# Five placeholder entries taken out of the order of work of a hybrid decoder step

## The chip, the cores and the metric

The kernel runs on one core of a Trainium2 chip. Its time is the device time of one execution, in microseconds (us). Five engines work side by side, each in the order of its own list of instructions: TensorE (PE, matrix products), VectorE (DVE), ScalarE (ACT), GpSimd (POOL, which here issues the gathers) and SyncE (SP, which issues the loads of weights). They wait for each other by semaphores.

## The reference

One layer is computed for 576 tokens: 512 of a new sequence (the prompt) and 8 tokens each of 8 running sequences (the sample, 64 tokens). All numbers are float32.

- Mixer: z = x·w_in + b_in is cut into u, q, k, v and two gates. u goes through a state-space scan (S5), a GELU and a gated linear unit (GLU). q, k and v go through attention over a window of 128 keys. The two branches, each times the sigmoid of its gate, are added and multiplied with w_out.
- A layer norm of (alpha·x + mixer) gives x1.
- PEER, the channel mixer: each token makes 8 queries (x1·peer_wq), scores each against two sets of 128 keys, takes the best 16 pairs per head, and so has 128 experts of 16384. For each expert e it computes a = gelu(U[e]·x1)·gate and adds a·V[e]. U[e] and V[e] are rows of 1024 numbers, of the token's own choice.
- A second layer norm of (alpha·x1 + PEER) gives the output.

Each of the 576 tokens needs its own 128 rows of U and 128 rows of V.

## The kernel before

The tokens lie in five tiles: tile 0 is the sample (64 tokens), tiles 1 to 4 are the prompt (128 tokens each). They are worked in the order 1, 0, 2, 3, 4. Group 0 is tiles 0 and 1, group 1 is tiles 2, 3 and 4: the mixer runs once for each group.

PEER goes by slots. A slot is one expert of each of the 128 tokens of a tile: a gather of 128 U rows and a gather of 128 V rows (524 KB each). Tile 0 folds its 64 tokens twice into 128 partitions and so has 64 slots; the others have 128, together 576. For slot q:

- POOL issues the gather of U rows and, four slots behind, that of V rows (`u_row`, `v_row`, lines 683 and 696), each into a place of a ring. In slots 72 to 191 of the whole row of slots the ring of U has 6 places and that of V has 6. POOL waits until the place's former row has been used. Its instructions run in order, so a V gather that waits holds up the U gathers behind it.
- DVE forms the dot products with x1 (line 1513). After every fourth slot ACT does the GELU and DVE multiplies with the gate (`gated`, line 1482).
- The V row is weighed and added in one of two ways: ACT builds a diagonal matrix (line 1804) and PE multiplies it with the row (`weigh`, line 1038), or DVE adds it alone (`add_row`, line 1501, the first of a tile line 1497). `rows_on_vector` chooses which.

Two slots are a half-step, an item `("peer", t, c)` of tile t. While the slots of tiles 1 and 0 are worked (192 slots, 96 half-steps), the mixer of group 1 and the choice of experts of later tiles are worked between them. This is the mixed stage. Half-steps are counted through here, 0 to 63 for tile 1 and 64 to 95 for tile 0. After it only PEER of tiles 2 to 4 is left, with little between.

The order of the mixed stage is written in `schedule` as a list `mix` of entries, and spread by a planned cost: `COST` holds for every kind of item a time on DVE and one on PE. All costs of `mix` and `tops` are added and divided by `SPREAD` (184 slots); an entry goes in as soon as the costs placed so far, with half of its own, are within this rate times the number of slots. `("wait",)` is an entry that no engine has a function for: it does nothing, costs 4.0 in the sum, and so leaves about a slot free of mixer work.

From that one list each engine takes its own order. On PE `mixer_first` puts the items that follow a half-step ahead of that half-step's products with V rows. On DVE `half_steps_behind` puts items behind by a number of half-steps (`VECTOR_BEHIND`): `qkv` and `merge` by 2, `drain_wo` and `ln` by 1. On ACT most are one behind.

The items that matter here, in their order:

- `qkv` t: products for q, k, v (line 841 on PE), then bias and rotary embedding on DVE (lines 1219 to 1231). `turn` t: PE turns q and k over (lines 849, 852), and waits for the rotary embedding; ACT copies the results out of the banks (line 1574). `s`, `p`, `pt`, `pv`: attention (lines 900, 910, 920 on PE).
- `gs`, `ga`, `merge` m, for eight m: gates, GLU and the branch of attention (line 933 on PE, lines 1319 to 1330 on DVE).
- `wo` k, for eight k: the product with w_out for tiles 2 and 3 in four banks (line 961). The first waits until DVE has done the last merge. `drain_wo` (line 1358) adds a finished bank to x on DVE. `wo_last` 4: the two halves of tile 4 (line 971); the first goes into the bank of `wo` 2,0 and waits until DVE has drained it.
- `ln` t (lines 1339 to 1352), `xt` t: PE turns x1 over (line 981) and waits for `ln` t. `wq` h, for eight h: the queries (line 990); they need all three `xt`.
- `last` 1: DVE's sum of the rows that it added is folded into the bank by PE (line 1052). `final` 1: the second norm of tile 1 on DVE (lines 1538, 1339 to 1352).

Of the kernel before, what the change touches and what calls it, by code (L numbers as in the profile page):

```python
# [93 lines left out]
def schedule():  # L94

    gates = lambda m: [("gs", 0, m), ("ga", 0, m)]
    s = [("tables",), ("u",), ("ut",), ("uc",), ("qkv", 0), ("ca", 0), ("qkv", 1), ("ca", 1), ("wt",),
         ("turn", 0), ("turn", 1), ("ws",), ("rec",), ("k", 0), ("k", 1),
         ("ss",)] + gates(0) + gates(1) + gates(2) + gates(3)
# [3 lines left out]
    wo = lambda t, hf: [("wo_last", t, hf), ("drain_wo", t, hf)]  # L103
# [4 lines left out]
    first = [[("top", 1, 2)], [("top", 1, 3)], [("choose", 1, 1), ("sc", 1, 2)], [("index", 1, 1)]]  # L108
    first += [[("top", 1, h)] for h in range(4, 8)] + [[("choose", 1, 2)], [("index", 1, 2), ("sc", 0, 0)]]
    parts = [(j, kv) for j in range(1, 4) for kv in range(2)]  # L110
    attention = [[("qkv", 2)], [("qkv", 3)], [("qkv", 4)], [("wait",)], [("turn", 2), ("turn", 3), ("turn", 4)], [("s", *parts[0])], [("p", *parts[0]), ("s", *parts[1])]]
    for n in range(1, len(parts)):
        attention.append([("pt", *parts[n - 1]), ("p", *parts[n])])
        attention.append([("pv", *parts[n - 1])] + ([("s", *parts[n + 1])] if n + 1 < len(parts) else []))
# [1 line left out]
    mix = [first[0], attention[0], first[1], first[2], attention[1], first[3]]  # L116
    first, attention = first[4:], attention[2:]
# [3 lines left out]
            mix.append(first[n])  # L121
    for m in range(8):
        mix += [[("gs", 1, m)], [("ga", 1, m)], [("merge", 1, m)]]
    mix += [[("wait",)]] + [[("wo", k)] for k in range(8)]
    mix += [[("drain_wo", 2, 0), ("drain_wo", 2, 1)], [("wait",)], [("wo_last", 4, 0)], [("ln", 2)], [("wo_last", 4, 1)]]
    mix += [[("drain_wo", 3, 0), ("drain_wo", 3, 1)], [("ln", 3)], [("drain_wo", 4, 0), ("drain_wo", 4, 1), ("xt", 2)], [("ln", 4)], [("xt", 3)]]
    mix += [[("wait",)], [("wait",)], [("wait",)], [("xt", 4)], [("wait",)]] + [[("wq", 1, h)] for h in range(8)]
    mix += [[("sc", 2, 0), ("sc", 2, 1)], [("wait",)]] + [[("top", 2, h)] for h in range(2)] + [[("choose", 2, 0)], [("index", 2, 0)]]
    tops = [[("top", 0, h)] for h in range(4)] + [[("choose", 0, 0), ("sc", 0, 1)], [("index", 0, 0)]]
    tops += [[("top", 0, h)] for h in range(4, 8)] + [[("choose", 0, 1)], [("index", 0, 1), ("fold",)]]  # L130
# [171 lines left out]
class Plan:  # L302
# [3 lines left out]

    def __init__(self):
        self.items = schedule()
        self.on_vector = rows_on_vector(self.items)
        self.filled, self.drained, self.before, self.bank = {}, {}, {}, {}  # L310
# [1632 lines left out]
```

## Time and profile before

| what | value |
|---|---|
| median of 3 runs | 2052.76 us (2048.89 to 2058.01) |
| profiled execution | 2049.74 us, span 2047.9 us |
| PE busy | 1589.3 us, 78% of the span |
| DVE busy | 1246.9 us, 61% |
| POOL busy | 1229.6 us, 60% |
| ACT busy | 439.3 us, 21% |
| read from HBM | 669.71 MB, 329 GB/s over the span |
| mean granted clock of PE | 0.866 of full speed |

"Busy" is the time in which an engine executes an instruction; issuing, waiting for semaphores and branching are not counted. The DMA share is the mean busy share of the core's 16 DMA engines. A matrix product in float32 with 128x128 weights and 512 columns appears as two instructions. One V row (one slot) on PE is two such products, one for each half of the 1024 columns, so four instructions of line 1038.

### The profile page before, as it was taken

To read this page: it belongs to the slowest core of one execution; us is meant where nothing else is said; L and a number is where in the kernel's file an instruction comes from. 1 tells how busy PE (TensorE), PEld (TensorE's weight loads), DVE (VectorE), ACT (ScalarE), POOL (GpSimd) and SP (SyncE) were. 2 spreads that over 40 slices of the span, in tenths; PEclk is the share of its full clock that TensorE was granted. 3 is DMA by queue.
4 is the path that set the end of the run, shared out by engine and by line. 5 is a ranking of instruction groups with operands and counts; after the bars stand their busy time and mean duration, and the time that the engine had idled before them with its cause. 6 is when DMAs were issued, how large, how long until landed. Compare 5 with 4: busy or idle time off the path is not lost.

```text
span 2047.9 us, 17225 instructions
## 1 busy us (share of the span) xinstructions
PE 1589.3 (78%) x4837; PEld 797.7 (39%) x4837; DVE 1246.9 (61%) x3135; ACT 439.3 (21%) x1035; POOL 1229.6 (60%) x1370
## 2 busy tenths in 40 slices
PE   7988887889989797973757767848868676687776
PEld 6787464445444432421323322313323222232222
DVE  7921448887697777567867547545756425444444
ACT  2342111462333213111111112211202111111110
POOL 0181056565776667676666667666767665666663
PEclk9988979889999998986869898859878788788878
DMA  5453389897999999899999998999999998999995
GB/s 216 139 153 91 119 335 356 321 338 278 340 407 397 397 381 387 293 351 362 352 363 372 389 356 347 362 366 383 357 375 369 380 365 321 373 361 370 380 360 224
DMA packets 186702, 675.10 MB, mean 330 GB/s; under 512 B 20976, under 2 KB 23456, under 8 KB 186192
## 3 DMA queue, kind: packets, MB, share of 16 engines
q0 software_dynamic: 167056, 609.25, 78.9%
q1 hardware_dynamic: 17632, 59.51, 8.2%
q10 hardware_dynamic: 1920, 5.24, 0.7%
q8 instruction: 40, 0.66, 0.1%
q14 instruction: 54, 0.44, 0.1%
HBM read 669.71 MB, written 3.69 MB: 329 GB/s over the span
## 4 chain that ended last, share of the span: by engine, by line
PE 46%; issue 17%; DVE 16%; POOL 8%; DMA 6%; another core or an unknown queue 5%; ACT 2%; ACTq 0%; SPq 0%; DVEq 0%; POOLq 0%
PE bank L1038 30%; DVE region L1513 3%; POOL region L683 3%; PE bank L933 3%; DVE wring L1513 2%; DMA wring<-in_pu,region 2%; POOL region L696 2%; DMA small<-in_pv,region 2%; PE first_banks L933 2%; POOL wring L683 1%; PE bank L737 1%; PE first_banks L990 1%; DVE region L1501 1%; PE bank L990 1%
## 5 line engine op out<-in xcount | busy, mean ns | idle before, releaser
L1038 PE MATMUL bank<-region,small 128*128 128x512 f32 (+1 forms) x728 | 382.6, 665 | 143.8 <-issue 79.5
L696 POOL DMA_INDIRECT region<-in_pv,region x320 | 323.2, 1010 | 185.5 <-issue 82.5
L683 POOL DMA_INDIRECT region<-in_pu,region x298 | 317.3, 1065 | 179.2 <-issue 83.7
L1513 DVE CUSTOM_DVE_ANT_0 wring<-wring,first_banks 128x1024 f32<-128x1024 f32 x228 | 272.8, 1218 | 154.4 <-DMA wring<-in_pu,region 113.0
L683 POOL DMA_INDIRECT wring<-in_pu,region x278 | 273.4, 983 | 121.4 <-issue 79.9
L1038 PEld LDWEIGHTS bank<-region,small 128*128 128x128 f32 (+1 forms) x728 | 143.1, 202 | 362.1 <-issue 299.4
L1038 PE MATMUL bank<-region 128*128 128x512 f32 x364 | 197.1, 662 | 103.6 <-issue 102.1
L1513 DVE CUSTOM_DVE_ANT_0 region<-region,first_banks 128x1024 f32<-128x1024 f32 x156 | 187.0, 1218 | 78.2 <-DMA region<-in_pu,region 57.3
L1513 DVE CUSTOM_DVE_ANT_0 region<-region 128x1024 f32<-128x1024 f32 x142 | 171.8, 1225 | 42.3 <-DMA region<-in_pu,region 39.5
L1804 ACT ACTIVATE small<-small,region 128x128 f32<-128x128 f32 (+1 forms) x317 | 105.3, 385 | 386.5 <-remote 128.2
L1038 PEld LDWEIGHTS bank<-region 128*128 128x128 f32 x364 | 75.5, 209 | 213.7 <-issue 209.0
L1812 ACT ACTIVATE region<-region 128x4 f32<-128x4 f32 x144 | 29.3, 203 | 530.5 <-DVE region L1513 323.7
L1804 ACT ACTIVATE region<-small,region 128x128 f32<-128x128 f32 x188 | 63.1, 392 | 245.2 <-remote 107.5
L696 POOL DMA_INDIRECT xT<-in_pv,region x80 | 77.2, 965 | 51.0 <-remote 25.2
L1482 DVE TENSOR_TENSOR region<-region 128x4 f32<-128x4 f32 x144 | 23.0, 160 | 112.9 <-issue 91.5
L1038 PE MATMUL bank<-xT,small 128*128 128x512 f32 x168 | 82.4, 633 | 10.9 <-issue 10.5
L1038 PE MATMUL bank<-xT,region 128*128 128x512 f32 x152 | 76.5, 647 | 13.4 <-issue 13.3
L1513 DVE CUSTOM_DVE_ANT_0 wring<-wring,region 128x1024 f32<-128x1024 f32 x50 | 61.3, 1227 | 27.5 <-DMA wring<-in_pu,region 24.3
L933 PE MATMUL bank<-xT,wring 128*128 128x192 f32 (+1 forms) x336 | 77.4, 388 | 0.0
L696 POOL DMA_INDIRECT discretisation<-in_pv,region x48 | 50.6, 1055 | 40.8 <-PE bank L1038 21.8
L1501 DVE SCALAR_TENSOR_TENSOR region<-region 128x1024 f32<-128x1024 f32 x46 | 59.2, 1287 | 21.7 <-issue 12.3
L1038 PE MATMUL bank<-discretisation,small 128*128 128x512 f32 (+1 forms) x112 | 60.4, 661 | 10.6 <-issue 6.9
(371 smaller groups left out, 2391.0 us busy)
## 6 DMA issues: line engine op xcount, KB each, us to landing
wring<-in_w SPq DMA_DIRECT2D x100, 512.0 KB, 5.2
region<-in_pv,region POOLq DMA_INDIRECT x320
region<-in_pu,region POOLq DMA_INDIRECT x298
wring<-in_pu,region POOLq DMA_INDIRECT x278
region<-in_w SPq DMA_DIRECT2D x4, 512.0 KB, 5.0
small<-in_small ACTq DMA_DIRECT2D x1, 1669.0 KB, 8.3
xT<-in_xT SPq DMA_DIRECT2D x1, 1536.0 KB, 12.6
region<-in_x SPq DMA_DIRECT2D x3, 512.0 KB
```

The lines of the kernel that those rows point to most:

```text
L683: pool.indirect_dma_start(ring_u[u_at.place[q]], None, io["pu"], bass.IndirectOffsetOnAxis(ind[:, k:k + 1], 0)).then_inc(g_u[u_at.place[q] ...
L696: pool.indirect_dma_start(ring_v[v_at.place[q]], None, io["pv"], bass.IndirectOffsetOnAxis(ind[:, k:k + 1], 0)).then_inc(g_v[v_at.place[q] ...
L737: last = mm(b[:, 0:cn], w[:, k, :], xT[:, k, c0:c0 + cn], start=k == 0, stop=k == KT - 1)
L933: last = mm(b[:, 0:cn], w[:, k0 + k, :], src[:, k, s0:s0 + cn], start=k == 0, stop=k == kn - 1)
L990: last = mm(b[:, 0:cn], w[:, k, :], xT[:, k, c0:c0 + cn], start=k == 0, stop=k == KT - 1)
L1038: last = mm(bank[6 + hf][0:tn, :], diagonal[diag_at[d]][:, 0:tn], ring_v[v_at.place[q]][:, 512 * hf:512 * hf + 512], start=k == 0, stop=t ...
L1482: V.tensor_tensor(aact[:, n % 2, k], hact[:, n % 2, k], gt[:, k], ALU.mult).then_inc(a_s, 1)
L1501: V.scalar_tensor_tensor(out=acc, in0=ring_v[v_at.place[q]], scalar=aact[:, n % 2, k:k + 1], in1=acc, op0=ALU.mult, op1=ALU.add).then_inc( ...
L1513: V.tensor_tensor_reduce(out=ring_u[u_at.place[q]], in0=ring_u[u_at.place[q]], in1=first_banks[:, :] if t > 1 else x1[t], scale=1.0, scala ...
L1804: S.activation(diagonal[diag_at[d]][:, 0:tn], eye, ACT.Copy, scale=aact[:, n % 2, k:k + 1]).then_inc(diag_s, 1)
L1812: S.activation(hact[:, n % 2, k], hdot[:, n % 2, k], ACT.Gelu).then_inc(act_s, 1)
```

## The change

Five of the eight `("wait",)` entries of `mix` are taken out: the one ahead of `turn`, the one ahead of `wo` 0, the one between `drain_wo` 2 and `wo_last` 4,0, and two of the three between `xt` 3 and `xt` 4. Where the third stood, `wo_last` 4,0 becomes part of the entry of `drain_wo` 2. Nothing that is computed changes.

```diff
-    attention = [[("qkv", 2)], [("qkv", 3)], [("qkv", 4)], [("wait",)], [("turn", 2), ("turn", 3), ("turn", 4)], [("s", *parts[0])], [("p", *parts[0]), ("s", *parts[1])]]
+    attention = [[("qkv", 2)], [("qkv", 3)], [("qkv", 4)], [("turn", 2), ("turn", 3), ("turn", 4)], [("s", *parts[0])], [("p", *parts[0]), ("s", *parts[1])]]
...
-    mix += [[("wait",)]] + [[("wo", k)] for k in range(8)]
-    mix += [[("drain_wo", 2, 0), ("drain_wo", 2, 1)], [("wait",)], [("wo_last", 4, 0)], [("ln", 2)], [("wo_last", 4, 1)]]
+    mix += [[("wo", k)] for k in range(8)]
+    mix += [[("drain_wo", 2, 0), ("drain_wo", 2, 1), ("wo_last", 4, 0)], [("ln", 2)], [("wo_last", 4, 1)]]
     mix += [[("drain_wo", 3, 0), ("drain_wo", 3, 1)], [("ln", 3)], [("drain_wo", 4, 0), ("drain_wo", 4, 1), ("xt", 2)], [("ln", 4)], [("xt", 3)]]
-    mix += [[("wait",)], [("wait",)], [("wait",)], [("xt", 4)], [("wait",)]] + [[("wq", 1, h)] for h in range(8)]
+    mix += [[("wait",)], [("xt", 4)], [("wait",)]] + [[("wq", 1, h)] for h in range(8)]
```

## Rows read from the trace of the kernel before

**Rows 1.** The page: the span, and busy time of each engine.

```profile
span 2047.9 us, 17225 instructions
PE 1589.3 (78%) x4837; PEld 797.7 (39%) x4837; DVE 1246.9 (61%) x3135; ACT 439.3 (21%) x1035; POOL 1229.6 (60%) x1370
```

**Rows 2.** Windows: busy us (instructions) of PE, PEld, DVE, ACT, POOL; clock, DMA share, GB/s.

```profile
303.00:348.00 45.00, 44.82 (x141) 23.62 (x140) 43.42 (x131) 7.06 (x17) 32.46 (x30) 1.00 0.92 339
348.00:361.00 13.00, 0.87 (x6) 0.66 (x5) 8.29 (x39) 2.02 (x6) 6.81 (x7) 0.67 1.03 412
...
550.00:608.00 58.00, 55.79 (x160) 29.74 (x159) 50.14 (x139) 17.05 (x26) 42.30 (x38) 1.00 1.02 408
608.00:703.00 95.00, 78.78 (x218) 41.88 (x217) 75.78 (x137) 29.80 (x42) 62.56 (x54) 0.93 1.03 402
...
775.00:815.00 40.00, 28.02 (x71) 10.00 (x72) 27.28 (x47) 15.55 (x34) 27.33 (x26) 0.87 1.00 394
815.00:871.00 56.00, 56.00 (x168) 28.01 (x168) 32.52 (x46) 5.60 (x15) 34.46 (x30) 1.00 0.86 302
...
914.00:2048.00 1134.00, 797.00 (x1618) 324.11 (x1616) 626.87 (x1577) 173.36 (x513) 735.27 (x769) 0.81 0.94 358
```

**Rows 3.** Timeline of PE, turn: start, us, instruction, [idle before <-releaser].

```profile
348.04 0.27 PE L852 MATMUL first_banks<-small,region 128*128 128x128 f32 x1
360.44 1.08 PE L849 MATMUL first_banks<-small,region 128*128 128x128 f32 x4 [12.13 <-ACT region L1574]
...
361.53 9.26 PE L1038 MATMUL bank<-region,small 128*128 128x512 f32 x16
```

**Rows 4.** Timelines of ACT and POOL around the same place.

```profile
359.12 0.69 ACT L1804 ACTIVATE small<-small,region 128x128 f32<-128x128 f32 x2 [10.17 <-DVE region L1482]
...
359.29 1.76 POOL L683 DMA_INDIRECT region<-in_pu,region  x1 [3.83 <-DVE region L1513]
365.43 1.95 POOL L696 DMA_INDIRECT region<-in_pv,region  x1 [4.38 <-DVE region L1513]
```

**Rows 5.** Timeline of PE from the last merge of group 1 to `wo_last`.

```profile
700.93 5.32 PE L933 MATMUL bank<-hgT,wring 128*128 128x384 f32 x16
706.09 2.74 PE L933 MATMUL first_banks<-region,wring 128*128 128x384 f32 x8
711.99 1.98 PE L1038 MATMUL bank<-region,small 128*128 128x512 f32 x4 [3.16 <-issue]
715.58 1.98 PE L1052 MATMUL bank<-region,small 128*128 128x512 f32 x4 [1.60 <-DVE region L1501]
717.40 1.02 PE L961 MATMUL first_banks<-wring,region 128*128 128x512 f32 x2
...
728.24 3.62 PE L1038 MATMUL bank<-region,small 128*64 128x512 f32 x8 [0.38 <-ACT small L1804]
```

**Rows 6.** Timeline of DVE in the same stretch.

```profile
708.78 0.62 DVE L1319 SCALAR_TENSOR_TENSOR region<-bank,small,region 128x384 f32<-128x384 f32 x1 [2.97 <-issue]
...
714.24 1.28 DVE L1501 SCALAR_TENSOR_TENSOR region<-region 128x1024 f32<-128x1024 f32 x1
...
733.15 0.75 DVE L1497 TENSOR_SCALAR region<-small,region 128x1024 f32<-128x1024 f32 x1 [1.13 <-issue]
```

**Rows 7.** Timeline of POOL: gathers of V rows of tile 0.

```profile
731.03 1.80 POOL L696 DMA_INDIRECT region<-in_pv,region  x1 [0.30 <-issue]
...
734.39 0.94 POOL L696 DMA_INDIRECT region<-in_pv,region  x1 [0.30 <-issue]
...
741.06 1.86 POOL L696 DMA_INDIRECT discretisation<-in_pv,region  x1 [4.48 <-PE bank L1038]
```

**Rows 8.** Timeline of PE: `xt` and the first `wq` of group 1.

```profile
792.07 1.08 PE L981 MATMUL first_banks<-small,region 128*128 128x128 f32 x4 [7.62 <-issue]
...
805.67 5.34 PE L1038 MATMUL bank<-region,small 128*64 128x512 f32 x8 [3.60 <-ACT small L1804]
...
815.55 5.43 PE L990 MATMUL first_banks<-xT,wring 128*128 128x384 f32 x16
```

## The prediction

> **What bounds the kernel now.** First the page: no engine is busy over 78% of the span [rows 1], so the bound has to be looked for by stage. Next the windows. After 914 us only PEER is left: 1134 us at a DMA share of 0.94 and 358 GB/s [rows 2]. The reader is to see that this half is a matter of gathers; the change does not touch it, so it is taken as it is, later or earlier by whatever the mixed stage gains or loses. The mixed stage, 258 to 914 us, has no single bound. From 550 to 703 us the DMA engines are full (share 1.02 and 1.03, 408 and 402 GB/s), while PE has idle time. From 775 to 815 us they are as full (1.00, 394 GB/s) and PE is busy for 28.02 of 40 us. From 815 to 871 us, the eight `wq`, it is the reverse: PE is busy for 56.00 of 56.00 us, and the DMA share falls to 0.86 [rows 2]. The third view is the timeline at the places of the five entries. There PE stands still for another engine: 12.13 us ahead of `turn` 4, 7.62 us ahead of `xt` 3, 3.60 us ahead of the rows before `xt` 4 [rows 3, 8].
>
> **What the planner does with it.** The costs of `mix` and `tops` add up to 548.1 planned us before and 528.1 after (five times 4.0 less); over 184 slots that is a rate of 2.98 and 2.87 per slot. I worked the placing rule through for both lists. Entries behind the first removed one come a half-step earlier at first (`turn` from 11 to 10, `s` 1,0 from 13 to 12), are level around half-step 20, then fall behind, by 1 to 2 from 28 to 65 (`merge` 1,7 from 63 to 65, `wo` 0 from 65 to 66, `wo` 7 from 69 to 70, `wo_last` 4,0 stays at 71), and are back at 77 (`ln` 4 at 77 for 76, `xt` 4 at 78 for 79, `wq` 0 at 79 for 80, `wq` 1 and all later at their old places). Seven more V rows go from PE to DVE by the same lists: one in tile 1, four net in slots 0 to 31 of tile 0 (12 for 8), two in its slots 32 to 63. No instruction is added or lost beyond that exchange, and no DMA: the same 50 pieces of weights are loaded by SP in the same order, some of them later.
>
> **Part 1, `turn` (half-steps 10 to 13).** PE's 12.13 us ahead of `turn` 4 are a wait for a bank. ACT empties it, and ACT was itself behind diagonals whose gates come after DVE's next dot products (10.17 us) [rows 3, 4]. With `turn` a half-step earlier ACT has it ahead of those diagonals, so that the copies can start at once and PE goes on with V rows. POOL was held up there by 3.83 us (a U place) and 4.38 us (a V place that row 18 on PE frees) [rows 4]. What goes on PE is worth at most what POOL waits, since around it the DMA engines are full (1.03 [rows 2]): between 0 and 8.2 us. The U wait is DVE's own load and largely stays; I take the V wait and round it: −4.
>
> **Part 2, the end of tile 1.** Now DVE waits 2.97 us for the last merge, and does it in four instructions of about 0.6 us (2.4 us) [rows 6]. Afterwards merge 6 stands there, whose products are long done: the 2.97 us go, the 2.4 us stay. One row more is added by DVE (the row that PE does at 711.99 [rows 5]), 1.4 us from start to start. Net −1.5. Pieces of weights for the last merge and for `wo` come later, past a stretch with full DMA queues: each is 0.524 MB, at 402 GB/s 1.3 us; none to four of them, 0 to −5, and I take −1, because what is put off has to be loaded a few half-steps later. Together −2.5.
>
> **Part 3, `wo` 0 behind the last merge.** Here lies the cost. `merge` 1,7 is now behind `last` 1. On PE it takes 7.9 us (5.32 and 2.74 for its 24 instructions [rows 5]) from about 716.0, so until 723.9. `wo` 0 waits until DVE has done that merge, and on DVE it stands two half-steps later: behind four dot products, `final` 1 (6.3 us), four more dot products, and two rows of the tile (0.75 and 1.28 us [rows 6]). Counted from the trace of before, less the 1.5 us of part 2, DVE reaches it at about 732.7 and ends at 735.1. So `wo` 0 starts at 735.1 instead of 717.40 [rows 5]: PE is 17.7 us of work behind, with some 11 us of it idle. Queued behind the waiting `wo` 0 are the products with V rows 0 and 1 of tile 0 (at 728.24 before [rows 5]), and behind them on POOL the V gather that needs row 0's place: it goes from 731.03 to about 741, and the U gathers behind it too. Part of that was waited anyway, 4.48 us two rows later [rows 7], for a place that row 2 frees; this row is now DVE's.
>
> What gives it back: four rows less on PE, 1.81 us each (3.62 for two [rows 5]), 7.2 us; and PE's own idle time later, 7.62 and 3.60 us [rows 8] and 1.1 us ahead of a row at 775, 12.3 us. What adds: `wo_last` 4,0 waits for DVE to drain `wo` 2,0, which now comes behind the dot products of half-step 72 instead of 70; the gather of the last of these is some 9.6 us late, and PE waits about 3.8 us with two half-steps of rows behind it. 17.7 + 3.8 − 7.2 − 12.3 = +2.0 at `xt` 4. Bounds: −2 if the wait at `wo_last` does not come about, +14.3 if none of the idle time can be used, since it is itself a wait for `ln` behind late dot products.
>
> **Part 4, `xt` 4 and `wq`.** `xt` 4 stands a half-step earlier than its `ln` allows: PE waits for `ln` 4 with rows 24 and 25 behind it, and not with 26 and 27. From its end the eight `wq` (5.43 us for each [rows 8]) and nine rows are left as before, and two rows fewer in the middle: 3.6 us less, of which the late V places on POOL take a part. −2, between −3.6 and +3.6.
>
> **Part 5, two effects of the chip.** A gather beside DVE's additions can take longer: 1.80 us at 731.03, but 0.94 us at 734.39 [rows 7]. Seven more additions cost POOL between 0 and 7 times 0.86, 6 us; most gathers stay at 0.94, so +1. The clock of PE is 0.67 in the window with the 12.13 us of idle time, that is partly at the lower of its two levels, and four rows then take 9.26 us instead of 7.2 [rows 2, 3]. That one dip goes, those of the two `xt` waits shrink, two new idle stretches around 701 to 714 and 724 to 735 us bring one each: 0, between −2 and +4.
>
> The Trainium skill has a rule for either. "SBUF — State Buffer", section "SBUF: two separate sides", says that VectorE and GpSimd share one pair of ports by an exclusive lock, in which the loser stands still for a whole instruction; but that a VectorE instruction with two SBUF inputs holds it only against a GpSimd instruction that reads SBUF. By the first half every added row could cost its 1.28 us, 9 us in all; by the second, nothing, if issuing a gather does not read. The rows show both durations and leave it open. "TensorE: Matmul & The Clock Gate", section "What's actually happening", says that an idle array goes to half its clock and that activity brings it back; the clock of 0.67 beside the idle stretch agrees.
>
> **The sum.** −4 − 2.5 + 2.0 − 2 + 1 + 0 = −5.5 us, of the mixed stage and so of the whole: the profiled execution's 2049.74 would be 2044.2. It lies 3.0 below the median of its runs; from the median it is 2047.3, and I say 2048. About 0.5%, 10.3 us, is what a measurement here can tell from no change, so "same" is 2042.5 to 2063.0.
>
> **Rivals.** *A, the transfers take it all:* wherever PE or DVE gains, the DMA engines are full (1.02, 1.03, 1.00 [rows 2]), and the saved waits turn into waits for gathers. For it: at 348 to 361 us PE does nothing, yet the DMA share is 1.03. Against: 0.92 just before and 0.86 in `wq`. Time 2053. *B, slower:* the wait ahead of `wo` 0 is not given back. With 6 places the V ring of tile 0 runs dry while PE waits, POOL stands with it, and what DMA time is lost here can't be made up, since 394 to 408 GB/s is all that it reaches. Place: half-steps 66 to 78. Price: +14.3 for part 3, +3.6 for part 4, +2 for clock and ports, and −4 as parts 1 and 2 give less than hoped: +16, 2068. It decides from the point where `xt` 4 starts over 8 us later than now, counted from `last` 1. For it: POOL's waits for PE there are already 4.48 us long [rows 7]. Against: PE is busy for only 28.02 of 40 us from 775 on [rows 2]. *C, much faster:* the 8.2 us of part 1 and the 1.5 and 5 of part 2 come in full, part 3 is given back, part 4 gives 2: −16.7, 2036. *That the change does nothing at all* is out, as the orders differ.
>
> **Chances.** My forecast 0.45, with 2041 to 2056 as its own range; A 0.17; B 0.18; C 0.20. The range for all is 2037 to 2065: it leaves out about half of B and of C. Faster by over 0.5%: most of C and a little of mine, 0.21. Slower by over 0.5%: B less its mild end and a little of mine, 0.17. Same: 0.62.
>
> **What would show it.** In the profile after: ahead of `turn` 4 no wait of PE over 3 us; DVE's 2.97 us ahead of the last merge of tile 1 gone; 24 instructions of line 933 behind line 1052, and then 9 to 13 us of PE idle time ahead of the first line 961, released by DVE line 1330; a POOL gather of V right after it with a wait of some 8 us or more; a shorter wait ahead of `xt` 3; the end of the eighth `wq` within 5 us of where it was, counted from line 1052; the span after the mixed stage at 1134 us, within 3. The prediction is wrong in its main step if POOL loses more than 10 us between `last` 1 and `wq` 7, and wrong in its frame if the part after the mixed stage changes by more than the mixed stage does.

## The result and the profile after

The changed kernel takes 2064.94 us (median of 20 runs, 2051.34 to 2075.82), the kernel before 2057.03 us beside it (20 runs, 2043.86 to 2062.61). The ratio is 1.0051, 95% interval 1.0032 to 1.0070: slower by half a percent, some 10 us. The forecast was 5.5 us the other way. The profiled execution of the changed kernel took 2072.2 us, 7 above the median, which has to be kept in mind below.

The page, which answers to [rows 1]: fewer instructions on PE (V rows moved to DVE), yet more busy time.

```profile
span 2070.4 us, 17167 instructions
...
PE 1605.5 (78%) x4809; PEld 803.0 (39%) x4809; DVE 1253.4 (61%) x3142; ACT 441.7 (21%) x1030; POOL 1226.1 (59%) x1370
```

Windows of the kernel after, columns as in [rows 2]: busy us (instructions) of PE, PEld, DVE, ACT, POOL; clock, DMA share, GB/s.

```profile
703.00:745.00 42.00, 28.37 (x69) 13.48 (x68) 35.63 (x55) 11.40 (x17) 22.44 (x20) 0.84 0.96 362
745.00:775.00 30.00, 27.95 (x64) 11.53 (x63) 20.11 (x27) 1.24 (x5) 21.77 (x20) 0.97 0.88 313
775.00:815.00 40.00, 31.92 (x82) 11.76 (x80) 27.93 (x46) 11.37 (x23) 31.13 (x28) 0.97 0.97 367
815.00:871.00 56.00, 51.47 (x142) 24.90 (x143) 37.36 (x55) 9.04 (x23) 32.67 (x30) 0.92 0.93 341
...
924.00:2060.00 1136.00, 817.79 (x1614) 329.85 (x1613) 618.61 (x1566) 174.56 (x511) 731.21 (x768) 0.80 0.94 357
```

The same first two windows of the kernel before:

```profile
703.00:745.00 42.00, 36.86 (x89) 15.45 (x88) 35.35 (x53) 10.03 (x17) 27.40 (x24) 1.00 0.99 384
745.00:775.00 30.00, 29.28 (x67) 10.96 (x65) 20.32 (x34) 3.51 (x10) 20.99 (x22) 1.00 0.98 360
```

The reader is to see where PE loses work: 8.5 us of busy time in 703 to 745 us, at a clock of 0.84 for 1.00. The DMA engines follow one window later: share 0.88 for 0.98, 313 for 360 GB/s. That is 47 GB/s over 30 us, 1.4 MB or not quite three gathers of 524 KB, on top of 0.9 MB in the window ahead.

Timeline of PE after, the places of [rows 5, 8]: start, us, instruction, [idle before <-releaser].

```profile
715.41 3.58 PE L1052 MATMUL bank<-region,small 128*128 128x512 f32 x4 [5.25 <-DVE region L1501]
718.83 5.32 PE L933 MATMUL bank<-hgT,wring 128*128 128x384 f32 x16
723.99 2.74 PE L933 MATMUL first_banks<-region,wring 128*128 128x384 f32 x8
735.11 2.07 PE L961 MATMUL first_banks<-wring,region 128*128 128x512 f32 x2 [8.38 <-DVE region L1330]
736.98 2.96 PE L961 MATMUL bank<-wring,region 128*128 128x512 f32 x4
...
740.73 3.65 PE L1038 MATMUL bank<-region,small 128*64 128x512 f32 x8
...
772.72 7.08 PE L971 MATMUL first_banks<-wring,region 128*128 128x512 f32 x12 [2.06 <-DVE region L1358]
...
805.15 0.63 PE L981 MATMUL first_banks<-small,region 128*128 128x128 f32 x4 [3.10 <-DVE region L1358]
...
819.53 1.12 PE L981 MATMUL bank<-small,region 128*128 128x128 f32 x4 [9.51 <-DVE region L1352]
```

The last merge (24 instructions of line 933) now stands behind `last` 1 (line 1052), and `wo` 0 (line 961) waits 8.38 us for DVE line 1330, the last instruction of that merge. The first two V rows of tile 0 follow at 740.73. DVE over the same stretch shows why the merge took so long to come:

```profile
707.14 0.61 DVE L1319 SCALAR_TENSOR_TENSOR region<-bank,small,region 128x384 f32<-128x384 f32 x1
...
712.65 2.70 DVE L1501 SCALAR_TENSOR_TENSOR region<-region 128x1024 f32<-128x1024 f32 x2
...
719.85 1.40 DVE L1538 SCALAR_TENSOR_TENSOR region<-region,bank 128x512 f32<-128x512 f32 x2
...
724.93 1.28 DVE L1352 SCALAR_TENSOR_TENSOR region<-region,stat 128x1024 f32<-128x1024 f32 x1
...
732.68 0.60 DVE L1319 SCALAR_TENSOR_TENSOR region<-bank,small,region 128x384 f32<-128x384 f32 x1
...
734.50 0.56 DVE L1330 TENSOR_TENSOR region<-region 128x384 f32<-128x384 f32 x1
```

PE's part of the merge was done by 726.7 (723.99 + 2.74); DVE reached it only behind `final` 1 (719.85 to 726.21) and the dot products and rows after it. POOL paid for the wait, and DVE's dot products paid for POOL's. First POOL after (compare [rows 7], 4.48 us), then DVE after, just ahead of `xt` 4:

```profile
742.93 0.94 POOL L696 DMA_INDIRECT region<-in_pv,region  x1 [12.37 <-PE bank L1038]
...
760.44 0.94 POOL L696 DMA_INDIRECT region<-in_pv,region  x1 [2.74 <-PE bank L1038]
...
825.13 0.94 POOL L696 DMA_INDIRECT region<-in_pv,region  x1 [9.69 <-PE bank L1038]
```

```profile
808.75 1.23 DVE L1513 CUSTOM_DVE_ANT_0 region<-region 128x1024 f32<-128x1024 f32 x1 [3.02 <-DMA region<-in_pu,region]
...
813.40 1.23 DVE L1513 CUSTOM_DVE_ANT_0 region<-region 128x1024 f32<-128x1024 f32 x1 [3.34 <-DMA region<-in_pu,region]
...
818.19 1.28 DVE L1352 SCALAR_TENSOR_TENSOR region<-region,stat 128x1024 f32<-128x1024 f32 x1
```

The last line is `ln` 4; `xt` 4 starts 1.3 us after it begins. Counted from `last` 1, `ln` 4 ends 15.8 us later than before (104.1 for 88.3). Part of that is its place: the change has it a half-step, two dot products, further back in DVE's list. The rest is lateness that came by way of the gathers: the two dot products ahead of it wait for U gathers that POOL issued 10.9 and 11.6 us later than before. PE meets `ln` 4 at all because the change has `xt` 4 a half-step earlier; `xt_later` below takes these two apart.

Where the lateness begins is seen at POOL's gathers of U rows. The last one ahead of the V gather that waits 12.37 us is issued 0.2 us earlier than before, the next one 11.0 us later. Before:

```profile
728.76 1.97 POOL L683 DMA_INDIRECT region<-in_pu,region  x1 [0.30 <-issue]
...
733.14 0.94 POOL L683 DMA_INDIRECT region<-in_pu,region  x1 [0.30 <-issue]
```

After:

```profile
728.59 1.97 POOL L683 DMA_INDIRECT region<-in_pu,region  x1 [0.30 <-issue]
...
744.17 0.95 POOL L683 DMA_INDIRECT region<-in_pu,region  x1 [0.30 <-issue]
```

These are slots 138 and 139, counted from 0 over tiles 1 and 0. The difference is 10.9 us at slot 156, swings between 20.0 (slot 166) and 4.2 us (slot 184) behind it, and is 9.1 us at slot 192, the first of tile 2. So a lateness as large as the whole loss of the mixed stage is there behind this one wait.

Counted from `last` 1 (line 1052) in each profile, in us:

| point | before | after | difference |
|---|---|---|---|
| first `wo` | 1.8 | 19.7 | +17.9 |
| `wo_last` 4,0 | 39.2 | 57.3 | +18.1 |
| `xt` 3 | 76.5 | 89.7 | +13.2 |
| `xt` 4 | 95.4 | 104.1 | +8.7 |
| end of the eighth `wq` | 154.9 | 165.7 | +10.8 |
| first dot product of tile 2 | 205.2 | 214.6 | +9.4 |

Up to `last` 1 there is no difference (715.58 and 715.41 us). Behind the mixed stage the two profiled executions differ by another 13 us (1117.8 and 1131.1 us from tile 2's first dot product to PE's end). The change is not likely to be its cause: the median ratio is worth 10 us in all, and in the experiments below that part lies between 999.0 and 1001.4 us in all twelve profiles, whatever was done to the mixed stage. What made it differ here is not shown.

### The profile page after: what moved, and what is told of

It is laid out like the page before. It is cut to its first block, busy times and chain, and to the rows that moved or that the text cites. A ratio compares the mean times of both kernels' runs of the same rounds, so it can differ in the third digit from the quotient of the medians.

```text
span 2070.4 us, 17167 instructions
## 1 busy us (share of the span) xinstructions
PE 1605.5 (78%) x4809; PEld 803.0 (39%) x4809; DVE 1253.4 (61%) x3142; ACT 441.7 (21%) x1030; POOL 1226.1 (59%) x1370
## 4 chain that ended last, share of the span: by engine, by line
PE 51%; issue 17%; DVE 14%; POOL 7%; DMA 5%; another core or an unknown queue 3%; ACT 2%; ACTq 0%; DVEq 0%; SPq 0%; POOLq 0%
PE bank L1038 35%; DVE region L1513 3%; PE bank L933 3%; POOL region L696 2%; POOL region L683 2%; DMA small<-in_pv,region 2%; DMA region<-in_pu,region 1%; DVE wring L1513 1%; POOL wring L683 1%; DMA wring<-in_pu,region 1%; PE first_banks L933 1%; PE bank L737 1%; PE bank L990 1%; PE bank L841 1%
## 5 line engine op out<-in xcount | busy, mean ns | idle before, releaser
L696 POOL DMA_INDIRECT region<-in_pv,region x320 | 328.3, 1026 | 237.2 <-remote 81.2
L1038 PE MATMUL bank<-region,small 128*128 128x512 f32 (+1 forms) x696 | 365.7, 670 | 101.6 <-issue 42.0
L683 POOL DMA_INDIRECT region<-in_pu,region x298 | 310.2, 1041 | 175.8 <-issue 83.8
L1038 PE MATMUL bank<-region 128*128 128x512 f32 x364 | 211.3, 704 | 92.5 <-issue 87.5
L1038 PEld LDWEIGHTS bank<-region 128*128 128x128 f32 x364 | 79.7, 221 | 218.1 <-issue 211.3
L1501 DVE SCALAR_TENSOR_TENSOR region<-region 128x1024 f32<-128x1024 f32 x54 | 69.5, 1286 | 29.5 <-issue 17.6
L1038 PE MATMUL bank<-wring,small 128*128 128x512 f32 x76 | 47.3, 720 | 28.2 <-issue 28.2
L1038 PE MATMUL bank<-wring,region 128*128 128x512 f32 x84 | 48.9, 678 | 24.3 <-issue 24.2
```

The costliest lines, as they stand in the source:

```text
L683: pool.indirect_dma_start(ring_u[u_at.place[q]], None, io["pu"], bass.IndirectOffsetOnAxis(ind[:, k:k + 1], 0)).then_inc(g_u[u_at.place[q] ...
L696: pool.indirect_dma_start(ring_v[v_at.place[q]], None, io["pv"], bass.IndirectOffsetOnAxis(ind[:, k:k + 1], 0)).then_inc(g_v[v_at.place[q] ...
L1038: last = mm(bank[6 + hf][0:tn, :], diagonal[diag_at[d]][:, 0:tn], ring_v[v_at.place[q]][:, 512 * hf:512 * hf + 512], start=k == 0, stop=t ...
L1501: V.scalar_tensor_tensor(out=acc, in0=ring_v[v_at.place[q]], scalar=aact[:, n % 2, k:k + 1], in1=acc, op0=ALU.mult, op1=ALU.add).then_inc( ...
```

## The experiments

The theory: the slower planned pace (rate 2.87 for 2.98) lets the last merge fall behind `last` 1; PE then waits at `wo` 0, the V ring runs dry, and the lost gathers aren't regained. The rivals: `xt` 4 a half-step too early; the exchange of rows between PE and DVE; the pauses themselves as places where V rows get by.

The runs were made on other chips, on which the kernel before takes 1911.96 to 1913.63 us. Ratios are to the kernel before on the same chip (6 to 12 runs of each kernel, 20 to 30 of the one before). A profiled execution can lie 7 us beside the median of its kernel (1907.16 and 1913.78 for `before_again`, 1918.55 and 1922.59 for `after_again`), so times of less than some 7 us are read from ratios alone, and the ends of stages in two profiles can't tell a gain of that size. Two helpers recur: `moved` takes an item to another place in the finished order, with the split of V rows left as planned; `ROWS_ON_VECTOR` fixes the split as a list.

**The two kernels again.** No edit in either.

> The kernel before itself, for a profile on the same chip and as a measure of what the comparison gives for no change: ratio 0.999 to 1.001 by every theory.

> The changed kernel once more, as the point of comparison on the chip that the experiments ran on, where the kernel before takes 1914 us and not 2057. If the loss is a wait of fixed length it is 8 to 12 us here as well, ratio 1.004 to 1.006; if it is lost DMA time it scales with the chip, ratio 1.005. Its mixed stage (to the first dot product of tile 2) should be 7 to 12 us longer than that of the kernel before, the rest of the span equal within 3 us.

Measured: 1.0004 (0.9994 to 1.0014) and 1.0056 (1.0042 to 1.0070). The loss is the same share of a time that is 7% shorter. PE of `after_again` shows the same two waits, and so does POOL:

```profile
700.69 3.78 PE L1052 MATMUL bank<-region,small 128*128 128x512 f32 x4 [8.80 <-DVE region L1501]
...
720.40 2.08 PE L961 MATMUL first_banks<-wring,region 128*128 128x512 f32 x2 [7.51 <-DVE region L1330]
...
804.95 1.11 PE L981 MATMUL bank<-small,region 128*128 128x128 f32 x4 [9.45 <-DVE region L1352]
```

```profile
729.10 0.94 POOL L696 DMA_INDIRECT region<-in_pv,region  x1 [13.26 <-PE bank L1038]
```

The stretch of 60 us from `last` 1 on, first in `before_again`, then in `after_again`: 53 GB/s less over 60 us are 3.2 MB, six gathers.

```profile
698.00:758.00 60.00, 58.95 (x134) 23.02 (x134) 47.62 (x75) 8.73 (x24) 41.57 (x36) 0.99 0.98 373
```

```profile
698.00:758.00 60.00, 48.64 (x104) 20.74 (x104) 43.57 (x64) 8.70 (x17) 34.06 (x29) 0.85 0.89 320
```

**The merge put back ahead of `last` 1**, everything else as after.

```diff
+        moved(s, ("merge", 1, 7), ("last", 1))
```

> The changed kernel, with merge 1,7 put ahead of last 1 again (where it stood before the change), and the split of V rows left as the change made it. Theory W (the wait ahead of the first wo is the loss): PE's 8.4 us wait ahead of line 961 falls to under 2 us, POOL's wait of 12.4 us for the V place of row 0 to under 5 us, and 7 to 11 us of the change's 8 to 10 us loss come back: ratio to the kernel before 0.999 to 1.002. Theory X (xt 4 stands too early, PE waits 9.5 us there with V rows behind it): the first waits go, but the eighth wq still ends some 10 us late, ratio 1.004 to 1.006. Theory S (seven more V rows on DVE are the loss): ratio 1.004 to 1.006.

Measured: 1.0028 (1.0017 to 1.0038), half of the loss, and less than the wait's theory said (0.999 to 1.002). The waits at `wo` 0 (7.51 us) and on POOL (13.26 us) are gone:

```profile
723.86 1.59 POOL L703 DMA_INDIRECT region<-in_pv,region  x1 [1.43 <-PE bank L1045]
```

But two merges now stand close together ahead of `last` 1, and DVE waits for PE at both (line numbers are 7 higher here):

```profile
697.70 0.62 DVE L1326 SCALAR_TENSOR_TENSOR region<-bank,small,region 128x384 f32<-128x384 f32 x1 [3.80 <-PE bank L940]
...
700.29 0.56 DVE L1336 TENSOR_TENSOR region<-first_banks,region 128x384 f32<-128x384 f32 x1 [1.38 <-PE first_banks L940]
```

`last` 1 comes at 707.27 us, for 700.69 in `after_again`. So the wait is one cause. In the profile the lateness has in part moved: the dot product right behind `last` 1 (slot 128) is 8.9 us later than in `before_again`, for 2.3 us in `after_again`. An order made for another pace isn't mended by one move.

**The merge put behind `last` 1 in the kernel before**: the order of the suspected cost alone, with the pauses kept.

```diff
+        moved(s, ("merge", 1, 7), ("wo", 0))
```

> The kernel before, all eight pauses in place, with only merge 1,7 moved from ahead of last 1 to just ahead of wo 0; the split of V rows as before. Theory W: PE waits 8 to 12 us ahead of the first line 961, and 6 to 12 us are lost: ratio 1.003 to 1.006. Theories X and S: nothing of theirs is touched, ratio 0.999 to 1.001.

Measured: 1.0080 (1.0063 to 1.0097), 14.7 us. One item in another place, in a kernel with all its pauses and its old pace, costs more than the whole change, and more than was expected (1.003 to 1.006). `wo` 0 follows the merge directly here, and not a half-step later as in the change. PE and POOL (line numbers 7 higher); POOL waits longer than in `after_again`:

```profile
713.80 2.07 PE L968 MATMUL first_banks<-wring,region 128*128 128x512 f32 x2 [8.32 <-DVE region L1337]
```

```profile
728.08 0.94 POOL L703 DMA_INDIRECT region<-in_pv,region  x1 [16.49 <-PE bank L1045]
```

It is also the cleanest test of the idle time that the prediction counted on, as the split and the place of `xt` 4 are those of before. Apart from the 8.32 us, PE's waits between `last` 1 and `xt` 4 add up to 11.6 us, for 10.5 in `before_again`, and `xt` 4 starts 112.7 us after `last` 1, for 93.7: nothing was given back.

**`xt` 4 and the first `wq` back to their half-steps**, the rest as after.

```diff
+        moved(s, ("xt", 4), ("peer", 0, 16))
+        moved(s, ("wq", 1, 0), ("peer", 0, 17))
```

> The changed kernel, with xt 4 and wq 0 of group 1 put a half-step later, where they stood before the change. Theory W: PE's wait ahead of xt 4 falls from 9.5 to under 4 us, but the rows that take its place were late anyway, so at most 2 us of time come back: ratio 1.004 to 1.006. Theory X: 7 to 10 us come back, ratio 0.999 to 1.002. Theory S: 1.004 to 1.006.

Measured: 1.0034 (1.0022 to 1.0045), below what the wait's theory said (1.004 to 1.006) and above the 0.999 to 1.002 of the other. PE's wait ahead of `xt` 4 is 0.1 us for 9.45, and the eighth `wq` ends 159.8 us after `last` 1 for 164.9; the wait at `wo` 0 stays (8.21 us). Between 1.0034 and 1.0056 lie 4.2 us, with intervals that just touch: by the ratios the earlier `xt` 4 is a second cost of the change, and not a gain. The profiles don't confirm it: tile 2's first dot product comes 207.0 us after `last` 1, for 205.9 in `after_again`. With `xt` 4 where it was before, PE's waits between `last` 1 and `xt` 4, without the one at `wo` 0, are 6.7 us for 10.5 in `before_again`: 3.8 us were given back.

**Both moves together.**

```diff
+        moved(s, ("merge", 1, 7), ("last", 1))
+        moved(s, ("xt", 4), ("peer", 0, 16))
+        moved(s, ("wq", 1, 0), ("peer", 0, 17))
```

> The changed kernel with merge 1,7 ahead of last 1 and xt 4 and wq 0 a half-step later. Theory WX (two waits with V rows queued behind, at wo 0 and at xt 4, one part each): ratio 0.998 to 1.001, 3 to 6 us below each of the two alone. Theory W: as merge_first, 1.002 to 1.004. If the waits are only where a general lateness of the mixer shows: as merge_first or worse.

Measured: 1.0022 (1.0011 to 1.0034). If the two gains added up in full it would be 1.0006, but with the intervals of all four ratios that can't be told from 1.0022; nor can `both_moved` be told from `merge_first`. What is left is 4.2 us. The mixer is still late in it: the last `wo` ends 44.0 us after `last` 1, for 35.7 before, and `last` 1 itself is as late as in `merge_first` (707.3 us, for 698.4 in `before_again`). That this is the reason was not tried.

**The split of rows.** First the changed kernel with the rows of the kernel before on DVE (46 of tile 1, 21 of tile 0); then the kernel before with those of the changed one (47 and 27); then the latter with the merge late too.

```diff
+ROWS_ON_VECTOR = {1: [6, 7, 11, ...], 0: [3, 4, 5, ...]}
+    out = {(t, k) for t, ks in ROWS_ON_VECTOR.items() for k in ks}
...
+    moved(s, ("merge", 1, 7), ("wo", 0))    # in the third kernel alone
```

> The changed kernel's order with the split of V rows between PE and DVE that the kernel before has (71 rows on DVE and not 78). Theory S: the loss goes, ratio 0.999 to 1.002. Theory W: PE has 7 rows more, 12.6 us, right where it is behind: no gain, or up to 8 us more lost, ratio 1.005 to 1.009. Theory X: as W, 1.005 to 1.009.

> The kernel before with nothing changed but the V rows that DVE takes: the 78 of the changed kernel for its own 71. Before the change PE has no wait at wo 0 to catch up with, but in tile 0 POOL waits for PE (4.1, 2.4, 3.6 and later 3.8, 3.7, 4.0 us): if rows on PE bound it there, 3 to 6 us are gained, ratio 0.997 to 0.9985. If DVE is as tight there, 0.999 to 1.001.

> The kernel before, all pauses in place, with two parts of the change alone: merge 1,7 behind final 1 (as in merge_late, 1.008) and the V rows split as after the change (78 on DVE). If the change is the sum of these two, its ratio of 1.0056: 1.004 to 1.007, 3 to 7 us below merge_late. If the split only helps the changed order: 1.007 to 1.009.

Measured: `split_of_before` 1.0091 (1.0074 to 1.0108), `split_of_after` 0.9971 (0.9954 to 0.9988), `late_and_split` 1.0043 (1.0027 to 1.0059). The exchange of rows, all seven, is the useful part of the change: taken back, the changed kernel loses another 6.7 us; given alone to the kernel before, it gains 5.7 us (1912.88 to 1907.16), and beats both kernels. In `split_of_after` POOL's wait at that place is small (line numbers 5 higher):

```profile
718.63 0.94 POOL L701 DMA_INDIRECT region<-in_pv,region  x1 [0.97 <-PE bank L1043]
```

The same kernel with the late merge is 12.6 us slower (1919.79), with the other split 14.7 us as seen, and POOL's wait is the longest of all kernels (17.99 us). Late merge and new split together give 1.0043, the change 1.0056, with intervals that overlap: these two parts account for the change within what can be measured.

**One pause alone**, the one ahead of `turn`, taken out of the kernel before.

```diff
-..., [("qkv", 4)], [("wait",)], [("turn", 2), ("turn", 3), ("turn", 4)], ...
+..., [("qkv", 4)], [("turn", 2), ("turn", 3), ("turn", 4)], ...
```

> The kernel before with one pause removed, the one ahead of turn; merge 1,7 and all from wo on stay at their half-steps, and one row more of tile 1 goes to DVE. By part 1 of the prediction the 12.13 us wait of PE falls below 6 us and 2 to 6 us are gained: ratio 0.997 to 0.999. By its rival A (full transfers take it back) 1.000. Theory W has no part in it: the wait ahead of wo 0 stays away, 0.999 to 1.001.

Measured: 1.0005 (0.9992 to 1.0018): nothing. The wait ahead of `turn` 4, expected under 6 us, is a microsecond shorter, first `before_again`, then `turn_only`:

```profile
354.73 1.08 PE L849 MATMUL first_banks<-small,region 128*128 128x128 f32 x4 [7.03 <-ACT region L1574]
```

```profile
350.33 1.09 PE L849 MATMUL first_banks<-small,region 128*128 128x128 f32 x4 [6.04 <-ACT region L1574]
```

The second starts 4.4 us earlier, and the first dot product of tile 2 is 3.4 us later in it (899.6 for 896.2): within what one execution scatters.

**Pauses and pace taken apart.** The changed kernel, without its five pauses, at nearly the pace of before (528.1 / 178 = 2.97); and the kernel before, with all pauses, at a slower pace (548.1 / 188 = 2.92).

```diff
-SPREAD = 184
+SPREAD = 178
```

```diff
-SPREAD = 184
+SPREAD = 188
```

> The changed kernel (five pauses out) with SPREAD 178 for 184, so that the planner's rate is 2.97 per slot as before the change (2.98) and merge 1,7 lands at half-step 63, ahead of last 1. The planner gives 46 + 15 + 11 rows to DVE. Theory P (the loss is the pace: a lower rate carried the last merge over the end of tile 1): the wait ahead of the first wo is gone and the time is that of the kernel before or less, ratio 0.997 to 1.001. If the missing pauses themselves cost (V rows behind waiting wo_last, xt, wq): 1.003 to 1.006, with PE waits of over 5 us ahead of wo_last or xt.

> The kernel before with all eight pauses and SPREAD 188 for 184: rate 2.92, merge 1,7 at half-step 64, behind last 1; 45 + 10 + 11 rows on DVE. Theory P: the wait ahead of the first wo appears here too (6 to 9 us of PE idle time), although no pause is missing: ratio 1.004 to 1.008. If missing pauses are the cause, 1.000 to 1.002.

Measured: `pace_kept` 0.9967 (0.9951 to 0.9984), `slow_pace` 1.0054 (1.0031 to 1.0077). With the pauses and a slow pace a loss as large as the change's is there; without the pauses and at the old pace there is a gain of 6.6 us, the fastest kernel of the study beside `split_of_after`. If the missing pauses cost anything by themselves, it is no more than what else `pace_kept` gained. PE of `pace_kept`: `wo` 0 follows `last` 1 at once.

```profile
693.76 3.78 PE L1052 MATMUL bank<-region,small 128*128 128x512 f32 x4 [0.72 <-DVE region L1501]
697.34 1.34 PE L961 MATMUL first_banks<-wring,region 128*128 128x512 f32 x2
...
732.47 6.89 PE L971 MATMUL first_banks<-wring,region 128*128 128x512 f32 x12 [5.13 <-DVE region L1358]
...
771.86 1.12 PE L981 MATMUL bank<-small,region 128*128 128x128 f32 x4 [1.03 <-DVE region L1352]
```

PE of `slow_pace`, where the merge has slipped to half-step 64, and POOL beside it (PE's wait was expected to be 6 to 9 us):

```profile
700.95 3.78 PE L1052 MATMUL bank<-region,small 128*128 128x512 f32 x4 [8.81 <-DVE region L1501]
...
716.58 2.07 PE L961 MATMUL first_banks<-wring,region 128*128 128x512 f32 x2 [4.12 <-DVE region L1330]
```

```profile
724.92 0.94 POOL L696 DMA_INDIRECT region<-in_pv,region  x1 [9.85 <-PE bank L1038]
```

Neither kernel changes one thing alone. `slow_pace` is late to the end of the mixed stage (`xt` 4 at half-step 80, the last `wq` at 89, for 79 and 87 before, while the change is back in step there). In its profile the dot products are 9.4 us later than in `before_again` at slot 184 and 19.0 us at slot 188, where `after_again` has 9.7 and 9.6: part of its loss is made there, and not at `wo` 0.

`pace_kept` has the old rate but 20 planned us less to place, so its mixer ends early (`xt` 4 at half-step 76, the last `wq` at 84). Its planner also gives DVE five more rows of tile 0 than before (26 for 21), and rows on DVE were seen to gain. POOL has a wait of 9.23 us in it too, ahead of the V row of slot 134. One long wait on POOL is therefore not by itself a loss. What `pace_kept` has not, and the slow kernels have, is that wait with the mixer late behind it; that this makes the difference is argued and not tried.

## Why the prediction was wrong, point by point

**Part 3, `wo` 0 behind the last merge: the step that failed.** Its first half came out nearly as worked: `wo` 0 at 735.11 (predicted 735.1), PE idle for 8.38 us (just under the 9 to 13), POOL waiting 12.37 us (8 or more), 2.06 us at `wo_last` (3.8). That 735.1 was met so closely is partly luck. DVE began its four dot products 0.17 us earlier than before and not 1.5, and two of its waits that the kernel before has there (0.87 and 1.13 us) were gone.

The second half failed: "PE's own idle time later, 7.62 and 3.60 us and 1.1 us", 12.3 us that were to be given back. In the changed kernel PE's waits between `last` 1 and `xt` 4, without the one at `wo` 0, are 14.7 us for 12.7 before. The wait ahead of `xt` 3 did shrink, 7.62 to 3.10 us, but 9.51 us stand ahead of `xt` 4. These places are not all waits for `ln`, as the prediction has it. `ln` 3 was done at 784.7 us before; what PE waited for until 792.07 is the bank that `xt` 3 writes, the one of `wo_last` 4,0, and DVE empties it with `drain_wo` 4,0, which stands behind a dot product that waits for its U gather. DVE before:

```profile
790.09 1.22 DVE L1513 CUSTOM_DVE_ANT_0 region<-region 128x1024 f32<-128x1024 f32 x1 [3.70 <-DMA region<-in_pu,region]
...
791.24 0.68 DVE L1358 SCALAR_TENSOR_TENSOR region<-region,first_banks 128x512 f32<-128x512 f32 x1
```

The 3.60 us before `xt` 4 were a wait for diagonals by ACT (line 1804) [rows 8], which also come behind dot products. So each of them ends with DVE's dot products, and the U gathers of these stand on POOL behind the V gather that waited for PE. What makes PE late makes their end late too. `xt` 4 came 8.7 us later instead of 2.0. The experiments show it with less mixed in: 11.6 us of such waits in `merge_late` for 10.5, and 6.7 in `xt_later`, so between nothing and 3.8 of 12.3 us came back.

The bound beside the term, +14.3 "if none of the idle time can be used, since it is itself a wait for `ln` behind late dot products", named the mechanism but for the `ln`; I chose the wrong end. By the prediction's own test, a start of `xt` 4 over 8 us later, rival B decides. The mechanism is B's, shown by `merge_late` (14.7 us lost by that order alone) and `merge_first` (POOL's wait gone, half of the loss back). B's size was too large, +16 for some 10. The prediction's other test, more than 10 us lost by POOL between `last` 1 and the last `wq`, stands at the edge: its U gathers are 11.0 us late behind the wait and 7.7 us at slot 176, near the end of the eighth `wq`.

**The pace.** That the removal slows the whole plan was in the prediction. Not in it was that the loss comes from this: with the pauses out and the pace held, `pace_kept` shows none. That the crossing of `last` 1 is what costs at the slower pace, `merge_late` and `late_and_split` say better than `slow_pace`.

**Part 1, −4:** measured nothing. PE's wait fell from 12.13 to 6.05 us in the profile and not under 3, and `turn_only` gives 1.0005. `last` 1 came no earlier either (715.41 for 715.58). On the first chip DVE's dot products do run ahead of those before for a while, by 6.0 us at slot 80 and 7.3 at slot 100, and by 0.2 at slot 128. That would be rival A's mechanism for this part, as the DMA share is 1.02 from 550 us on [rows 2]; but `after_again` is 3.5 us behind at slot 80 and 1.8 ahead at slot 100, so it may be the scatter of single executions.

**Part 2, −2.5:** DVE's 2.97 us ahead of the merge are gone as predicted, and the gain with them. `last` 1 waits 5.25 us for DVE's rows, for 1.60 before [rows 5]: more rows on DVE near the end of the tile, 2.70 us for the last two.

**The exchange of rows, counted at 7.2 us within part 3:** 5.7 us alone and 6.7 us in the changed kernel, for all seven rows, where part 3 counts four. About right, and it hid part of the cost.

**Part 4, −2:** the sign was wrong, within its bounds (−3.6 to +3.6). `xt` 4 a half-step early waits for `ln` 4 with two rows queued behind it; put back, 4.2 us return by the ratios. POOL shows 9.69 us of waiting at 825.13, just behind.

**Part 5, +1 and 0:** the seven more additions cost POOL nothing that can be seen: its 384 issues of gathers of tiles 1 and 0 take 432.1 us together, for 432.2 before. The clock cost more than 0: four instructions of line 1052 take 3.58 us after the 5.25 us idle, for 1.98 before, the first six of `wo` take 4.83 us, and 0.84 is granted over 703 to 745 us for 1.00. From 715.4 to 719.0 us it is 0.55 and from 735.1 to 740.0 us 0.59, so most of both stretches ran at the lower of the two levels, 1.2 GHz; before, 1.00 was granted from 715.5 to 722.0 us. The Trainium skill, "TensorE: Matmul & The Clock Gate", section "What's actually happening", says that an idle array falls to half its clock and has to earn the other back; the factor of 1.8 between 3.58 and 1.98 us agrees. Some 4 us on PE by these durations, not on top of the sum, since PE waits for DVE later in any case.

With part 3 at its measured +8.7 for +2.0, part 4 at +2 for −2 and parts 1, 2 and 5 at 0, the stage would be about +11; measured +9.2 to the first dot product of tile 2, and 0.5% in the ratio. The eighth `wq` ended 10.8 us later, for the 5 allowed. The test of the frame (the rest after the mixed stage within 3 us) failed in the first two profiled executions, by 13 us that no run explains, and holds in the experiments: 999.3 and 1000.2 us.

**What stays open:** why `merge_first` keeps half of the loss and `both_moved` 4 us of it; what the early `xt` 4 costs, where ratios and profiles disagree; and how much of `pace_kept`'s gain is its split. A kernel with both the old pace and the split of `pace_kept` fixed was not run.

## What to carry to other kernels

A placeholder in a plan that spreads work by its summed cost is part of the pace: to judge a pause, take it out and hold the pace, or you test both at once. When everything shifts by a step, look first for the item that crosses a boundary where the engines' orders differ (here the end of a tile, with a long norm on the engine that the next product waits for). Idle time of an engine may be counted as slack only if what it waits for doesn't hang on the chain that is getting late. And where rings are short and the DMA engines are near full, look at when the gathers are issued: here issues put off by 11 us were still 9 us late some fifty slots later.

## What the runs showed of the hardware

The same kernel takes 2057.03 us on one chip and 1912 to 1914 us on three others. Most of it, 118.5 of the 142.6 us between the two profiled executions, lies behind the mixed stage, where little but PEER is left: 1117.8 us and 999.3 us. The window of `before_again` there, to be read beside the last of [rows 2]:

```profile
896.00:1895.00 999.00, 758.64 (x1604) 285.00 (x1604) 622.80 (x1565) 169.01 (x511) 728.59 (x764) 0.94 1.02 404
```

404 GB/s at a DMA share of 1.02 for 358 at 0.94, with a granted clock of 0.94 for 0.81. DVE and POOL are busy for nearly as long in it (622.80 and 728.59 us, for 626.87 and 735.27); what differs is how fast gathers land. Whether it is the chip itself or something beside it isn't shown. The ratio of the change was the same on both, 1.0051 and 1.0056.
